# First modulation parts loaded and multiplied in pieces of 256 columns, with quarters of x and w_in; two modulation rows on GpSimd

## The reference

```python
c_act = jax.nn.silu(c)
mod = c_act @ w_ada[l] + b_ada[l]
sh1, sc1, g1, sh2, sc2, g2 = jnp.split(mod[:, None, :], 6, axis=-1)
h = x * (1.0 + sc1) + sh1
proj = h @ w_in[l]
u, cq, ckv, kr = jnp.split(proj, splits, axis=-1)
...
```

## Time and profile before

| what | value |
| --- | --- |
| three runs | 1521.86, 1524.03, 1528.92 us (median 1524.03) |
| profiled execution, device time | 1521.99 us |
| its span | 1520.2 us |
| mean granted TensorE clock | 0.994 |
| PE busy | 1491.9 us (98%) |
| DVE, POOL, ACT busy | 1204.8, 1019.9, 705.3 us |

### The profile page before, as it was taken

One profiled execution on the slowest core, in us unless ns is written; L12 is line 12 of the kernel. 1 busy time (PEld: TensorE's weight loads), 2 busy tenths in 40 slices (PEclk: granted clock), 3 DMA queues, 4 the chain that ended last, 5 costly groups with the idle time before them and its releaser, 6 DMA issues.

```text
span 1520.2 us, 21850 instructions
## 1 busy us (share of the span) xinstructions
PE 1491.9 (98%) x7983; PEld 1253.5 (82%) x7983; DVE 1204.8 (79%) x1979; ACT 705.3 (46%) x1312; POOL 1019.9 (67%) x620
## 2 busy tenths in 40 slices
PE   8999999999999999999999999999999999999997
PEld 4345784488899999999999999988888888888885
DVE  6869734536899899998888880189998898999998
ACT  2034653433444433488888883433333333333343
POOL 2610102654378888776777775699988888888966
PEclk8999999999999999999999999999999999999999
DMA  9987137133179898889999997799999999999981
GB/s 364 340 252 90 27 109 279 55 113 111 54 261 330 306 339 305 298 294 370 366 376 359 377 363 294 261 369 372 382 388 367 378 388 381 379 387 367 376 282 69
DMA packets 216599, 439.99 MB, mean 289 GB/s; under 512 B 38180, under 2 KB 128804, under 8 KB 214572
## 3 DMA queue, kind: packets, MB, share of 16 engines
q1 hardware_dynamic: 178764, 303.49, 57.2%
q0 software_dynamic: 36864, 134.23, 23.8%
q10 hardware_dynamic: 864, 0.86, 0.2%
HBM read 380.72 MB, written 56.64 MB: 288 GB/s over the span
## 4 chain that ended last, share of the span: by engine, by line
PE 87%; DVE 3%; ACT 2%; DMA 1%; SPq 0%; issue 0%; POOL 0%; DVEq 0%
PE ps L1841 12%; PE ps L1843 12%; PE ps L1842 11%; PE ps L1864 11%; PE ps L1866 11%; PE ps L1865 11%; PE ps L1510 2%; PE ps L1511 2%; PE ps L1512 2%; PE ps L1856 1%; PE ps L1857 1%; PE ps L863 1%; PE ps L895 1%; PE ps L1540 1%; PE ps L1352 1%; ACT ps L1214 1%
## 5 line engine op out<-in xcount | busy, mean ns | idle before, releaser
L1726 POOL TENSOR_TENSOR utl<-u_raw,uth 128x1024 fp32r<-128x1024 f32 x128 | 312.9, 2445 | 138.7 <-ACT uth L1745 120.4
L1841 PE MATMUL ps<-h2h,uth 128*128 128x384 f32 x1024 | 347.4, 339 | 2.2 <-POOL utl L1726 1.5
L1732 POOL TENSOR_TENSOR vl<-v_raw,vh 128x1024 fp32r<-128x1024 f32 x128 | 310.6, 2428 | 48.0 <-ACT vh L1745 46.3
L1843 PE MATMUL ps<-h2h,utl 128*128 128x384 f32 x1024 | 342.5, 334 | 0.0
L1842 PE MATMUL ps<-h2l,uth 128*128 128x384 f32 x1024 | 342.2, 334 | 0.0
L1864 PE MATMUL ps<-vh,wh 128*128 128x512 f32 x768 | 298.9, 389 | 0.0
L1865 PE MATMUL ps<-vl,wh 128*128 128x512 f32 x768 | 298.8, 389 | 0.0
L1866 PE MATMUL ps<-vh,wl 128*128 128x512 f32 x768 | 298.8, 389 | 0.0
L2057 DVE TENSOR_TENSOR w_f<-a_in,g_in 128x384 f32<-128x384 f32 x128 | 207.9, 1625 | 91.3 <-DMA a_in<-act_scr 90.0
L1745 ACT ACTIVATE vh<-v_raw 128x1024 fp32r<-128x1024 f32 x128 | 135.6, 1059 | 207.5 <-DMA v_raw<-in_peer_v 158.5
L1841 PEld LDWEIGHTS ps<-h2h,uth 128*128 128x128 f32 x1024 | 192.4, 188 | 2.7 <-POOL utl L1726 1.9
(11 more groups left out here) (373 smaller groups left out, 2243.8 us busy)
## 6 DMA issues: line engine op xcount, KB each, us to landing
u_raw<-in_peer_uT SPq DMA_DIRECT2D x128, 512.0 KB, 7.2
v_raw<-in_peer_v SPq DMA_DIRECT2D x128, 512.0 KB, 9.5
act_scr<-acts SPq DMA_DIRECT2D x64, 384.0 KB, 4.6
g_scr<-stage SPq DMA_DIRECT2D x12, 2048.0 KB, 9.5
g_in<-g_scr SPq DMA_DIRECT2D x32, 768.0 KB, 9.8
a_in<-act_scr SPq DMA_DIRECT2D x64, 384.0 KB, 9.3
w_ada<-in_w_ada SPq DMA_DIRECT2D x10, 2048.0 KB, 15.4
w_q<-in_peer_w_query SPq DMA_DIRECT2D x8, 1024.0 KB, 5.7
```

What stands on the lines that cost most here:

```text
L1726: tt(k.utl[b % 3][:, :, :].rearrange(f3), k.u_raw[:, b % 4].rearrange(f3), k.uth[b % 3][:, :, :].bitcast(F32).rearrange(f3), ALU.subtract) ...
L1732: tt(k.vl[:, n % 4], k.v_raw[:, n % 4], k.vh[:, n % 4].bitcast(F32), ALU.subtract).then_inc(k.vl_done, 1)
L1841: mm(o, hi, k.h2h[:, kt, SP:T], start=(kt == 0), stop=False)
L1843: ins = mm(o, lo, k.h2h[:, kt, SP:T], start=False, stop=(kt == DK - 1))
```

## The change

The parts 0 to 3 are now eight **pieces** of 256 columns (`PIECES`, in the order in which a first projection slice needs them), each one load, one set of 8 matmuls (`piece_row`), one ACT copy into one of four small buffers (`evac_piece`), and one pair of columns (`piece_columns`). x and w_in come in quarters of two kt slices, `modulate` works on a quarter, and `first_tiles` is cut into halves of three tiles with pieces between them. Five small loads move from ACT's queue into SP's. Ten extra warm-up matmuls stand before the first tiles. Rows 4, 5 and 6 stay on PE, rows 8, 10 and 11 are on DVE, and rows 7 and 9 are on POOL, which multiplies all 8 slices by c at once (128x4096) and folds them in halves (2048, 1024, 512). Loads of rows 10 and 11 and of the attention weights wait for other counts than before. ACT copies rows 5 and 6 out between the projection's tiles. The second block clears more semaphores.

```diff
-    k.modp = k.sb("modp", [P, 2, 512], 153)
+    k.modp = k.sb("modp", [P, 4, 256], 153)
...
+    k.acc_pool = k.sem("acc_pool")
...
     PART = [0, 2, 1, 3] + list(range(4, 12))
+    PIECES = [(0, 0), (1, 0), (0, 1), (1, 1), (2, 0), (3, 0), (2, 1), (3, 1)]
+    HALF = 256
+    ROWS_PE, ROWS_POOL, ROWS_DVE = (4, 5, 6), (7, 9), (8, 10, 11)
...
+        def load_piece(p):
+            i, half = PIECES[p]
+            at = PART[i] * 512 + half * HALF
+            if i == 3:
+                sp.wait_ge(k.mod_mm, 1 + PIECES.index((0, half)))
+            sp.dma_start(k.w_ada[:, i % 3, :, half * HALF:(half + 1) * HALF],
+                         w_ada[:, :, at:at + HALF]).then_inc((wa, wa_rest)[half][i % 3], 16)
+
         def load_w_ada(i):
-            if i >= 3:
-                sp.wait_ge(k.mod_mm, i - 2) if i < 11 else sp.wait_ge(k.mod_acc_ready, 1)
-            cols = slice(PART[i] * 512, (PART[i] + 1) * 512)
-            if i < 2:
-                sp.dma_start(k.w_ada[:, i, 0:4], w_ada[:, 0:4, cols]).then_inc(wa[i], 16)
-                sp.dma_start(k.w_ada[:, i, 4:], w_ada[:, 4:, cols]).then_inc(wa_rest[i], 16)
+            if i < 10:
+                sp.wait_ge(k.mod_mm, {4: 4, 5: 7, 6: 8, 7: 9, 8: 10, 9: 11}[i])
+            elif i == 10:
+                sp.wait_ge(k.acc_pool, 1)
             else:
-                sp.dma_start(k.w_ada[:, i % 3], w_ada[:, :, cols]).then_inc(wa[i % 3], 16)
-
-        def load_x(half):
-            sp.dma_start(k.hT[:, 4 * half:4 * half + 4, :], io["xT"][:, 4 * half:4 * half + 4, :]).then_inc(k.s_xt[half], 16)
+                sp.wait_ge(k.mod_acc_ready, 1)
+            sp.dma_start(k.w_ada[:, i % 3], w_ada[:, :, PART[i] * 512:(PART[i] + 1) * 512]).then_inc(wa[i % 3], 16)
...
-        load_w_ada(0)
-        load_w_ada(1)
-        load_x(0)
-        load_w_in(0)
-        load_w_ada(2)
-        load_w_in(1)
-        load_w_ada(3)
-        load_x(1)
-        load_w_in(2)
-        load_w_in(3)
+        po = io["positions"]
+        for two in range(4):
+            load_piece(2 * two)
+            load_piece(2 * two + 1)
+            load_x(two)
+            load_w_in(two)
+            if two == 0:
+                sp.dma_start(k.posi[:, :], bass.AP(po.tensor, po.offset, [[0, P], [1, T]])).then_inc(k.s_ropein, 16)
+                sp.dma_start(k.consts[:, :], io["rope_rows"]).then_inc(k.s_ropein, 16)
+            if two == 1:
+                sp.dma_start(k.c_lay[:, :, :, :], io["s5_c"]).then_inc(k.s_crep, 16)
+                sp.dma_start(k.bb[:, :, :, :], io["s5_b"]).then_inc(k.s_s5in, 16)
+        sp.dma_start(k.lncol[:, :, :], io["ln_cols"]).then_inc(k.s_lncol, 16)
         for i in range(4, 12):
             load_w_ada(i)
...
-        sp.wait_ge(k.mod_acc_ready, 2)
+        sp.wait_ge(k.acc_pool, 2)
...
-        sp.wait_ge(k.mod_acc_ready, 3)
+        sp.wait_ge(k.mod_acc_ready, 2)
...
-        act.dma_start(k.c_lay[:, :, :, :], io["s5_c"]).then_inc(k.s_crep, 16)
...
+        def evac_piece(p):
+            act.wait_ge(k.mod_mm, p + 1)
+            if p >= 4:
+                act.wait_ge(k.mod_cols, p - 3)
+            nc.scalar.activation(k.modp[:, p % 4, :], ps[:, 0, 0:HALF], ACT.Copy).then_inc(k.modp_evac, 1)
+
+        def evac_row(i):
+            act.wait_ge(k.mod_mm, 9 + ROWS_PE.index(i))
+            nc.scalar.activation(k.mod_acc[:, (i - 4) * 512:(i - 3) * 512], ps[:, 0, :], ACT.Copy).then_inc(k.modp_evac, 1)
+
+        for p in range(4):
+            evac_piece(p)
...
-        for i in range(2, 7):
-            evac_row(i)
+        for p in range(4, 8):
+            evac_piece(p)
+        evac_row(4)
 
         act.wait_ge(k.seq_out, 1)
         act.wait_ge(k.pow_done, 1)
         act.wait_ge(k.xchain_done, 1)
         for dst, _, bank in FIRST:
+            if bank == 2:
+                evac_row(5)
+                act.wait_ge(k.seq_out, 2)
+                nc.scalar.activation(k.kr4[:, :], ps[:, 7, :], ACT.Copy).then_inc(k.kr_ready, 1)
+            elif bank == 3:
+                evac_row(6)
...
+            if i == 0:
+                continue
...
         ins.then_inc(k.xchain_done, 1)
+        pool.wait_ge(k.ccol_ready, 1)
+        for i in ROWS_POOL:
+            pool.wait_ge(wa[i % 3], 16 * (i // 3 + 1))
+            w = k.w_ada[:, i % 3]
+            step(nc.gpsimd.tensor_tensor(w, w, k.ccol[:, :].unsqueeze(2).broadcast_to([P, DK, 512]), ALU.mult))
+            for n in (DK // 2, DK // 4):
+                step(nc.gpsimd.tensor_tensor(w[:, 0:n], w[:, 0:n], w[:, n:2 * n], ALU.add))
+            nc.gpsimd.tensor_tensor(k.mod_acc[:, (i - 4) * 512:(i - 3) * 512], w[:, 0], w[:, 1], ALU.add).then_inc(k.acc_pool, 1)
...
-        def modulation(i):
-            dve.wait_ge(k.mod_cols, i + 1)
-            j = PART[i]
-            cols = slice(4 * j, 4 * j + 4)
-            step.tell(tt(k.modc[:, cols], ps[:, 7, cols], b_ada[:, cols], ALU.add), k.mod_read, i + 1)
-            if j in (2, 3):
+        def modulation(p):
+            dve.wait_ge(k.mod_cols, p + 1)
+            i, half = PIECES[p]
+            at = 4 * PART[i] + 2 * half
+            cols = slice(at, at + 2)
+            step.tell(tt(k.modc[:, cols], ps[:, 7, cols], b_ada[:, cols], ALU.add), k.mod_read, p + 1)
+            if at >= DK:
                 step(v.tensor_scalar(k.modc[:, cols], k.modc[:, cols], 1.0, None, ALU.add))
 
-        def modulate(half):
-            dve.wait_ge(k.s_xt[half], 16)
-            for kt in range(4 * half, 4 * half + 4):
+        def modulate(two):
+            modulation(2 * two)
+            modulation(2 * two + 1)
+            dve.wait_ge(k.s_xt[two], 16)
+            for kt in range(2 * two, 2 * two + 2):
                 v.tensor_scalar(k.hT[:, kt, :], k.hT[:, kt, :], k.modc[:, DK + kt:DK + kt + 1], k.modc[:, kt:kt + 1],
                                 ALU.mult, ALU.add).then_inc(k.ht_ready, 1)
...
+        modulate(0)
         dve.wait_ge(k.s_ropein, 32)
         step(v.tensor_copy(k.rtmp2[:, :], k.posi[:, :]))
         step(v.tensor_scalar(k.rtmp2[:, :], k.rtmp2[:, :], k.consts[:, 0:1], None, ALU.mult))
         reduce_angle(k.rtmp2[:, :], k.ang[:, :], k.rtmp[:, :], k.posi[:, :].bitcast(F32), k.rope_red)
 
-        modulation(0)
-        modulation(1)
-        modulate(0)
+        modulate(1)
...
+        modulate(2)
...
-        for j in range(3):
-            powers(j)
-        modulation(2)
-        powers(3)
-        modulation(3)
-        modulate(1)
-        for j in range(4, CH):
+        powers(0)
+        powers(1)
+        modulate(3)
+        for j in range(2, CH):
             powers(j)
...
-        for i in range(8, 12):
+        for i in ROWS_DVE:
...
         def modulation_row(i):
             pe.wait_ge(wa[i % 3], 16 * (i // 3 + 1))
-            if i >= 1:
...
+            pe.wait_ge(k.modp_evac, 8 + ROWS_PE.index(i))
+            row(i, slice(0, 512), 512)
+
+        def piece_columns(p):
+            i, half = PIECES[p]
+            pe.wait_ge(k.modp_evac, p + 1)
+            if p >= 1:
+                pe.wait_ge(k.mod_read, p)
+            for m in range(2):
+                at = 4 * PART[i] + 2 * half + m
+                ins = mm(ps[:, 7, at:at + 1], k.modp[:, p % 4, m * P:(m + 1) * P], k.ones[:, 0:1], start=True, stop=True)
             ins.then_inc(k.mod_cols, 1)
...
-        modulation_row(0)
-        modulation_columns(0)
-        modulation_row(1)
-        modulation_columns(1)
+        piece_row(0)
+        piece_columns(0)
+        piece_row(1)
+        piece_columns(1)
+        for _ in range(WARM // 2):
+            mm(ps[:, 6, 0:P], k.ident[:, :], k.ident[:, :], start=True, stop=True)
         first_tiles(0)
-        first_tiles(1)
-        modulation_row(2)
-        first_tiles(2)
-        modulation_columns(2)
-        modulation_row(3)
-        first_tiles(3)
-        modulation_columns(3)
-        for kt in range(4, DK):
-            ins = first_tiles(kt)
-            if kt < DK - 1:
-                modulation_row(kt)
-        ins.then_inc(k.seq_out, 1)
+        piece_row(2)
+        first_tiles(1, FIRST[:3])
+        piece_row(3)
+        piece_columns(2)
+        first_tiles(1, FIRST[3:])
+        piece_columns(3)
+        for two in (1, 2):
+            first_tiles(2 * two, FIRST[:3])
+            piece_row(2 * two + 2)
+            first_tiles(2 * two, FIRST[3:])
+            piece_row(2 * two + 3)
+            piece_columns(2 * two + 2)
+            first_tiles(2 * two + 1, FIRST[:3])
+            piece_columns(2 * two + 3)
+            first_tiles(2 * two + 1, FIRST[3:])
+        first_tiles(6)
+        modulation_row(4)
+        first_tiles(7).then_inc(k.seq_out, 1)
+        modulation_row(5)
...
             if i == 0:
-                pe.wait_ge(k.mod_read, 4)
+                pe.wait_ge(k.mod_read, 8)
...
-                modulation_row(7)
+                modulation_row(6)
...
-                                 k.kr_ready, k.rep_ready, k.mod_cols, k.mod_read, k.ht_ready, k.seq_evac]
```

(72 more changed lines are left out.)

5 lines of the change are left out of this document (removed).

## The result

Median 1551.08 us (1548.98 to 1554.49, 5 runs) against 1524.03 (1521.86 to 1528.92): ratio 1.0174, interval 1.0155 to 1.0193. The change makes the kernel slower by 27 us, inside the range, 5 us under the number forecast. The profiled execution took 1548.98 us, 27.0 more than that of before.

What follows compares the result with a forecast made beforehand. The first block's end, where PE and SP tie, was taken as the bound. It would move from 106.4 to 140 us (+33.6), plus 0.8 for clears: +34.4 on 1522.0 gives 1556 us, range 1537 to 1567.

Steps and rivals of the forecast that it cites:

- PE earlier: First block: pieces and quarters let PE start first_tiles(0) at 16.5 us, not 22.96, ending first tiles at 71.7, not 80.1.
- DVE order: First block: x chain starts at 39 us instead of 31.5 and ends about 70.5; powers(0) starts near 45.
- Row 7 blocks the powers: POOL's row 7, from 74 us, makes DVE's remaining powers wait for whole POOL instructions: pow_done at 96.5, not 78.
- The new wait: ACT's row 5 copy stands behind pow_done: PE idles from 75.5 to 97.5 us, then row 6 takes 3.7, to 101.
- Row 9 and SP: POOL's row 9 lands at 109 us, ends at 129.7; SP's 15 loads wait for it, 10.3 us, ending at 140.
- Clears: At the second block's start, clearing 13 more semaphores adds 0.75 us, and it shows in PE's wait.
- the price: POOL's rows at 2.39 ns an element: 7680 elements make 18.3 us a row.
- the gaps: Each gap between POOL's instructions lets one DVE instruction through: 4 x 0.38 us in row 7, three of 0.78 in row 9.
- the Trainium skill's factor of two: Alternative estimate for POOL's rows, about 2x slower than VectorE with two inputs: 22 us a row, sum 7 us more.
- the first (powers not blocked): Rival 1: POOL does not block DVE's powers, pow_done near 78 us, still slower at 1537 (range 1537 to 1550); chance 0.22.
- Its other price, 1547: Same rival's late-landing case: row 7 on POOL only starts at 79 us, with gaps for row 8, near 1547 us.

Runs made afterwards that it cites:

- dve_rows_in_psum: Changed kernel, ACT copying rows 5, 6 and kr before its powers wait, POOL's rows behind pow_done, DVE's rows accumulating in PSUM: 1546.7 us.
- pow_first: Changed kernel, with POOL made to wait for pow_done before row 7: 1547.7 us.
- copies_first: Changed kernel, with ACT's copies of rows 5, 6 and kr moved ahead of its wait for pow_done: 1561.3 us.

## Why the prediction was right

- **PE earlier.** first_tiles(0) at 16.69 (forecast 16.5), end of the first tiles 71.2 (71.7). The 1 KB loads cost nothing that PE saw: its one stop before row 6 was 1.11 us, for DVE's `hT` (forecast 1.2).
- **DVE order.** x chain 39.10 to 71.17 (39 to 70.5), powers from 45.4 (45).
- **Row 7 blocks the powers.** Begun at 75.10 (74), ten instructions of 128x256 left (11), four let through, pow_done 93.4 (96.5).
- **The new wait.** PE idle 19.9 us (22), row 6 3.50 us (3.7), ended at 98.25 (101).
- **Row 9 and SP.** Landed 106.27 (109), POOL done 122.36 (129.7), SP's 15 loads 11.1 us (10.3), block end at SP's 133.5 (140). DVE ended at 132.0 (139.5).
- **Clears.** 3.0 us instead of 1.7, +1.3 (forecast 0.75). It did not show as a stop: PE was itself 2.4 us later through the clock, which I had not forecast for the second block, and `ut` was there.

The block's end came 6.5 us before the 140 forecast, and that is the sum of errors both ways. POOL's two rows were 9.0 us shorter together (15.6 us instead of 20.0, 16.1 instead of 20.7). Against them stand 2.5 us: row 7 began 1.1 us later, SP's loads took 0.8 more, and the way from row 7's end to row 6's 0.5 more.

Two terms make up the 9.0. One is the price. I took 2.39 ns an element, from rows 1, for all 7680. The adds fit: 4.56 us for 2048 is 2.2 ns, 2.40 for 1024 is 2.3. The multiply by c, whose second input is one value repeated along 512 columns, took 7.08 us for 4096, 1.7 ns, instead of 9.8. Four instructions took 15.4 us instead of 18.3, twice: 6 us. Whether the repeated input or the operation makes it cheaper, no run shows. The other term is the gaps, 3 us: I had let POOL stand still while DVE did the one instruction that got in, 1.5 us in row 7 and 2.3 in row 9. It hardly did: in dve_rows_in_psum, where no row of DVE waits, the rows took 15.4 us each. The estimate by the Trainium skill's factor of two (22 us a row) was further off; against DVE's 5.97 us for a row of eight fused multiply-adds, POOL's 15.4 is 2.6 times.

Of the rivals, the first (powers not blocked) was refuted by the trace. The time alone would not have done it: 1551 is 1 us above the 1550 at which I had drawn the line between it and the forecast, and two of the five executions lie below that line. It was also mispriced: I gave it 1537, with POOL's rows free to run, but pow_first shows that DVE's row 8 takes the powers' place. Its other price, 1547 with row 7 at 79 and row 8 in the gaps, is close to what pow_first gave with row 7 at 78.40 (1547.7 us, 4.3 of it in the last expert stage). The forecast's own chain held, but copies_first shows I had not understood all of it: the stop of PE before row 6 was also what kept row 9 from following row 7 at once.

Not tried: a version in which SP issues w_qr ahead of row 11's load. How much of SP's 11 us could be hidden that way stays open.

## What to carry to other kernels

When work goes to POOL, read two things of every DVE instruction that will run beside it: whether both its full inputs lie in SBUF (or, for a multiply by one value such as `TENSOR_SCALAR`, its input and its output), and what hangs on its end. Where they do, each lasted in these runs until POOL's current instruction ended, whatever its own size; keep POOL's instructions short, order them behind the critical DVE work and whatever follows it, or put DVE's accumulator in PSUM. And in a queue with waits in a fixed order, such as SP's here, each load inherits the latest of all waits before it: look there first when an engine was freed and the end did not move.

## What the runs showed of the hardware

- In the changed kernel, a POOL multiply of 128x4096 with a repeated second input ran at 1.7 ns an element (7.08 us); adds of two full inputs at 2.2 to 2.3 (4.56 us for 2048, 2.40 for 1024).
- The first term of a DVE row, TENSOR_SCALAR of 128x512 from SBUF into SBUF (0.48 us, one tensor input), was blocked too: 4.80 us in pow_first. Into PSUM the same took 0.75 us and was not blocked (dve_rows_in_psum at 101.82, inside POOL's add that began at 100.95). The Trainium skill (the same section of "SBUF — State Buffer") has TENSOR_SCALAR among the operations with a fast mode that takes both port pairs; 0.48 against 0.75 us and the block that went with the 0.48 agree.
- In the changed kernel PE restarted at half clock behind idle times of 20 and 13 us (3.50 against 1.92 us; 6.90 against 4.53), which adds 1.6 and 2.4 us to a wait that is read only as its idle time.
